# Two token mixers and a mixture of experts on one core: the gated layer with v ahead of u, and 40 unread products in three waits of the routing

## The reference, cut to what matters

```python
# h: (256, 1024)
z = gelu(rms_norm(h, ln_mix) @ c_w_in)              # 1024 x 2048, exact gelu
u, v = split(z, 2)                                  # 1024 columns each
v = layer_norm(v, c_ln_g, c_ln_b)                   # over the 1024 columns of a row
# in chunks of 128 positions, 8 groups of 128 columns; w_s lower-triangular
vs = einsum('gts,bnsgc->bntgc', w_s * tril, v) + b_s
h = h + (u * vs) @ c_w_out                          # 1024 x 1024
xt = rms_norm(h, ln_ffn)
logits = xt @ router_w                              # 1024 x 8
gates = softmax(top_2(logits))                      # two of eight experts for a token
h = h + moe(xt, gates)                              # rows sorted by expert
```

## Time and profile before

| | us |
|---|---|
| median of 3 runs | 2088.61 |
| lowest and highest run | 2087.92, 2090.22 |
| the profiled execution | 2090.02 |
| its span | 2088.3 |
| TensorE busy in the span | 1965.2 (94%) |
| VectorE busy | 1592.8 (76%) |
| ScalarE busy | 1194.4 (57%) |
| GpSimd busy | 28.1 (1%) |

### The profile page before, as it was taken

The page is one execution under the profiler, slowest core; times in us unless marked ns, Lnnn a source line. Parts: engine busy times, 40 slices in busy tenths (PEclk is TensorE's granted clock), DMA queues, the critical chain, the costliest instruction groups (busy, mean ns, idle before and its releaser), DMA issues.

```text
span 2088.3 us, 27813 instructions
## 1 busy us (share of the span) xinstructions
PE 1965.2 (94%) x11046; PEld 1693.1 (81%) x11046; DVE 1592.8 (76%) x1997; ACT 1194.4 (57%) x1638; POOL 28.1 (1%) x32
## 2 busy tenths in 40 slices
PE   8999999978999999999999999798999999989998
PEld 7889997767878787878787877687789988868997
DVE  5868886557898989898989898667479984856655
ACT  4543445425777777777777776556344444644443
POOL 0000000000000000000000000000000000000000
PEclk9999999988999999999999999899899999999999
DMA  7348884525898889898989998243158973214551
GB/s 301 133 156 349 336 332 158 207 75 218 336 350 334 340 345 341 340 343 338 342 341 342 340 343 332 102 142 122 41 195 334 359 280 123 104 44 164 183 184 59
DMA packets 71405, 512.02 MB, mean 245 GB/s; under 512 B 8162, under 2 KB 8546, under 8 KB 9826
## 3 DMA queue, kind: packets, MB, share of 16 engines
q1 hardware_dynamic: 69536, 504.40, 64.2%
q10 hardware_dynamic: 1732, 5.77, 0.8%
HBM read 509.08 MB, written 1.05 MB: 244 GB/s over the span
## 4 chain that ended last, share of the span: by engine, by line
PE 81%; DVE 12%; ACT 4%; issue 2%; POOL 1%; DMA 0%; POOLq 0%; ACTq 0%; DVEq 0%
PE ps L517 24%; PE ps L519 23%; PE ps L518 23%; DVE w_lo L1268 6%; ACT w_hi L2084 2%; PE ps L901 1%; PE ps L730 1%; PE ps L682 1%; PE ps L526 1%; PE ps L696 1%; PE ps L788 1%; PE ps L919 1%; POOL stat L2507 1%; PE ps L534 1%; ACT score L2192 1%
## 5 line engine op out<-in xcount | busy, mean ns | idle before, releaser
L1268 DVE TENSOR_TENSOR w_lo<-ring,w_hi 128x1024 fp32r<-128x1024 f32 x862 | 1046.1, 1225 | 344.7 <-ACT w_hi L2084 317.7
L2084 ACT ACTIVATE w_hi<-ring 128x1024 fp32r<-128x1024 f32 x862 | 913.0, 1062 | 667.8 <-PE ps L519 660.8
L517 PE MATMUL ps<-w_hi,x_hi 128*128 128x512 f32 (+1 forms) x1056 | 407.9, 389 | 6.6 <-DVE x_lo L1548 4.7
L519 PE MATMUL ps<-w_hi,x_lo 128*128 128x512 f32 (+1 forms) x1056 | 400.5, 382 | 0.0
L518 PE MATMUL ps<-w_lo,x_hi 128*128 128x512 f32 (+1 forms) x1056 | 399.7, 381 | 0.0
L517 PE MATMUL ps<-x_hi,w_hi 128*128 128x256 f32 x1248 | 360.4, 289 | 4.4 <-DVE x_lo L1382 3.9
L518 PE MATMUL ps<-x_lo,w_hi 128*128 128x256 f32 x1248 | 356.1, 285 | 0.0
L519 PE MATMUL ps<-x_hi,w_lo 128*128 128x256 f32 x1248 | 355.8, 285 | 0.0
L517 PE MATMUL ps<-w_hi,h_hi 128*128 128x512 f32 x732 | 292.0, 399 | 18.7 <-DVE h_lo L1837 15.7
L518 PE MATMUL ps<-w_lo,h_hi 128*128 128x512 f32 x732 | 285.7, 390 | 0.0
L519 PE MATMUL ps<-w_hi,h_lo 128*128 128x512 f32 x732 | 285.1, 389 | 0.0
(11 more groups left out here) (265 smaller groups left out, 1444.9 us busy)
## 6 DMA issues: line engine op xcount, KB each, us to landing
ring<-in_stream SPq DMA_DIRECT2D x479, 1024.0 KB, 4.9
con<-in_consts ACTq DMA_DIRECT2D x1, 2048.0 KB, 23.2
arena<-in_ln_rows ACTq DMA_DIRECT2D x3, 512.0 KB, 3.9
resid<-in_x SPq DMA_DIRECT2D x1, 1024.0 KB, 6.3
arena<-in_fin_row ACTq DMA_DIRECT2D x2, 512.0 KB, 3.5
out<-rows SPq DMA_DIRECT2D x2, 512.0 KB, 2.6
arena<-in_w_s ACTq DMA_DIRECT2D x1, 512.0 KB, 5.7
con<-in_consts ACTq DMA_DIRECT2D x1, 237.0 KB, 4.1
```

The costliest lines, as they stand in the source:

```text
L517: pe.matmul(out_, lhs[0], rhs[0], start=start, stop=False)
L519: return pe.matmul(out_, lhs[1], rhs[0], start=False, stop=stop)
L1268: dve.tensor_tensor(lo, ring[:, q % RING, a:a + HALF], hi.bitcast(F32), ALU.subtract)\
L2084: act.activation(half_buffer(m)[0], ring[:, q % RING, a:a + HALF], ACT.Copy).then_inc(hi_ready, 1)
```

## The change

- The stream and the kernel take the columns of v first (banks 0 to 3), then those of u (banks 4 to 7).
- TensorE takes the spatial product of rows 0 to 127 after five of u's eight halves, and that of rows 128 to 255 after the last three halves of u for t = 0; the last three halves of u go by rows: t = 0 for all three, then t = 1. The gated rows are transposed by t (`gated_transposes`): those of t = 0 before the last half of u for t = 1, those of t = 1 ahead of the third half of w_out for t = 0. The first three halves of w_out go by rows too, t = 0 behind the wait for `catT_kept` 4, t = 1 behind 6; then two whole halves, then `last_rows`.
- VectorE puts its splits of u's halves between the steps of the layer norm and the gating, ScalarE between the pieces of gelu. Gelu, x_hi, x_lo and gating go by t. New semaphores are `u_first` (u complete for t = 0) and `gated` (rows gated, one for each t, in place of `heads_ready`).
- `keep_warm` is called in three more waits: 18 products before the transposes of norm 4, 4 between these and the router, 18 between the router and the ranks. Bank 2 takes them; nobody reads them.

```diff
--- before.py
+++ after.py
@@ -390,6 +390,8 @@
         ple_gated = sem("ple_gated")
         gelu_done = sem("gelu_done")
         vn_ready = sem("vn_ready")
+        u_first = sem("u_first")
+        gated = sem("gated")
         ws_masked = sem("ws_masked")
         spatial_ready = sem("spatial_ready")
         logits_ready = sem("logits_ready")
@@ -536,7 +538,7 @@
                 def scaled(n):
                     pe.wait_ge(rows_scaled, 3 * k + n)
 
-                if k in (1, 6, 7, 9):
+                if k in (1, 4, 6, 7, 9):
                     keep_warm(18, 2)
                 scaled(1)
                 for f in range(4):
@@ -860,9 +862,10 @@
             rowsT(3)
             pe.wait_ge(ada_taken, 2)
             row_product(W_CIN, 0)
-            row_product(W_CIN + 4, 4)
-            pe.wait_ge(ws_masked, 1)
-            for t in range(QB):
+
+            def spatial(t):
+
+                pe.wait_ge(ws_masked, 1)
                 pe.wait_ge(vn_ready, t + 1)
                 for half in range(2):
                     for i in range(4):
@@ -870,12 +873,52 @@
                         last = pe.matmul(ps[:, 2 * t + half, i * P:(i + 1) * P], ws[:, g, :],
                                          v_rows[:, t, g * P:(g + 1) * P], start=True, stop=True)
                     last.then_inc(spatial_ready, 1)
-            pe.wait_ge(heads_ready, 2)
-            cat_transpose(8)
-            pe.wait_ge(catT_kept, 6)
-            row_product(W_COUT, 4, branch=True)
+
+            def gated_transposes(t):
+
+                pe.wait_ge(gated, t + 1)
+                for half in range(2):
+                    for i in range(4):
+                        f = 4 * half + i
+                        last = pe.transpose(ps[:, 2 * t + half, i * P:(i + 1) * P], rows[:, t, f * P:(f + 1) * P], ident)
+                    last.then_inc(catT_ready, 1)
+
+            u0, c0 = 2 * (W_CIN + 4), 2 * W_COUT
+            for k in range(5):
+                row_tile(u0 + k, (x_hi[:, k, :], x_lo[:, k, :]), 4, k == 0, False)
+            spatial(0)
+            w = []
+            for t in range(QB):
+                for k in range(5, KT):
+                    if t == 0:
+                        w.append(half_slot(u0 + k, 1))
+                    if (t, k) == (1, KT - 1):
+                        gated_transposes(0)
+                    row_part(w[k - 5], t, (x_hi[:, k, :], x_lo[:, k, :]), 4, False, k == KT - 1)
+                    if t == 1:
+                        row_end[0].then_inc(half_done, 1)
+                if t == 0:
+                    row_end[0].then_inc(u_first, 1)
+                    spatial(1)
+            pe.wait_ge(catT_kept, 4)
+            w = []
+            for t in range(QB):
+                if t == 1:
+                    pe.wait_ge(catT_kept, 6)
+                for k in range(3):
+                    if t == 0:
+                        w.append(half_slot(c0 + k, 1))
+                    if (t, k) == (0, 2):
+                        gated_transposes(1)
+                    row_part(w[k], t, (x_hi[:, k, :], x_lo[:, k, :]), 4, k == 0, False)
+                    if t == 1:
+                        row_end[0].then_inc(half_done, 1)
+            for k in (3, 4):
+                row_tile(c0 + k, (x_hi[:, k, :], x_lo[:, k, :]), 4, False, False)
+            last_rows(c0 + 5, [(x_hi[:, k, :], x_lo[:, k, :]) for k in range(5, KT)], 4, False)
 
             rowsT(4)
+            keep_warm(4, 2)
             pe.wait_ge(gained, GAINED_AT[4] + 4)
             for t in range(QB):
                 for k in range(KT):
@@ -883,6 +926,7 @@
                                      col("router", k * 8, 8), start=k == 0, stop=k == KT - 1)
             last.then_inc(logits_ready, 1)
 
+            keep_warm(18, 2)
             pe.wait_ge(member_ready, 1)
             pe.matmul(ps[:, 1, 0:8], col("before"), member[:, 0, :], start=True, stop=True)
             pe.matmul(ps[:, 1, 8:16], col("before"), member[:, 1, :], start=True, stop=False)
@@ -1203,7 +1247,7 @@
                 pe.wait_ge(cmp_kept, l + 1)
                 attention_rest(parts, TAIL, 12, 5)
                 pe.wait_ge(mixed_kept, GROUP_BASE[1 + l] + 12)
-                pe.wait_ge(heads_ready, 3 + l)
+                pe.wait_ge(heads_ready, 2 + l)
                 cat_transpose(8)
                 pe.wait_ge(catT_kept, 10 + 4 * l)
                 row_product(n0 + B_OUT, 4, branch=True)
@@ -1536,6 +1580,14 @@
                                              scalar=gain, in1=hi.bitcast(F32), op0=ALU.mult, op1=ALU.subtract)\
                         .then_inc(catT_kept, 1)
 
+            def keep_gated(t):
+
+                for half in range(2):
+                    dve.wait_ge(catT_hi, 2 + 2 * t + half + 1)
+                    at = slice(None), slice(4 * half, 4 * half + 4), slice(t * P, (t + 1) * P)
+                    dve.tensor_tensor(x_lo[at], ps[:, 2 * t + half, :].rearrange("p (f s) -> p f s", f=4),
+                                      x_hi[at].bitcast(F32), ALU.subtract).then_inc(catT_kept, 1)
+
             def keep_cat(count, before, gain=None):
 
                 for n in range(count):
@@ -1743,23 +1795,31 @@
             norm(3, gain(3), next_half=2 * W_CIN + 1, between=both_columns)
             for i in range(2):
                 scale_columns(0, i)
-            slots_done(W_COUT)
+            u0 = 2 * (W_CIN + 4)
+            split_to(reach(u0))
             for t in range(QB):
-                dve.wait_ge(gelu_done, 4 + 2 * t + 2)
+                dve.wait_ge(gelu_done, 2 * t + 2)
                 for half in range(2):
                     ins = dve.bn_stats(bn[:, t, half, :], v_rows[:, t, half * BANK:(half + 1) * BANK])
                 link(ins)
                 link(dve.bn_aggr(mv[:, t, :], bn[:, t].rearrange("p a b -> p (a b)")))
                 link(dve.tensor_copy(stat[:, 8 + t:9 + t], mv[:, t, 1:2]))
-            root(stat[:, 8:10], 2, 1.0, LN_EPS)
+            dve.tensor_scalar(stat[:, 0:2], stat[:, 8:10], 1.0, LN_EPS, ALU.mult, ALU.add).then_inc(root_asked, 1)
+            roots[0] += 1
+            split_to(reach(u0 + 1))
+            dve.wait_ge(root_ready, roots[0])
             dve.wait_ge(ln_in, 16 * 3)
             for t in range(QB):
+                split_to(reach(u0 + 2 * t + 1))
                 link(dve.tensor_scalar(v_rows[:, t, :], v_rows[:, t, :], mv[:, t, 0:1], stat[:, t:t + 1],
                                        ALU.subtract, ALU.mult))
                 link(dve.tensor_tensor(v_rows[:, t, :], v_rows[:, t, :], ln_g, ALU.mult))
+                split_to(reach(u0 + 2 * t + 2))
                 dve.tensor_tensor(v_rows[:, t, :], v_rows[:, t, :], ln_b, ALU.add).then_inc(vn_ready, 1)
+            split_to(reach(u0 + 5))
             for t in range(QB):
                 for half in range(2):
+                    dve.wait_ge(gelu_done, 4 + 2 * t + half + 1)
                     dve.wait_ge(spatial_ready, 2 * t + half + 1)
                     for i in range(4):
                         g = 4 * half + i
@@ -1767,8 +1827,11 @@
                                                        in0=ps[:, 2 * t + half, i * P:(i + 1) * P],
                                                        scalar=col("bs", g, 1), in1=u_rows[:, t, g * P:(g + 1) * P],
                                                        op0=ALU.add, op1=ALU.mult)
-            ins.then_inc(heads_ready, 1)
-            keep_cat(4, 2)
+                ins.then_inc(gated, 1)
+                split_to(reach(u0 + 6 + 2 * t))
+                keep_gated(t)
+                if t == 0:
+                    split_to(reach(u0 + 7))
             add_branch(4, W_COUT + 4, first_half=1)
             norm(4, gain(4))
             dve.wait_ge(logits_ready, 1)
@@ -2297,14 +2360,36 @@
             act.dma_start(ln_g, ln_rows[0].partition_broadcast(P)).then_inc(ln_in, 16)
             act.dma_start(ln_b, ln_rows[1].partition_broadcast(P)).then_inc(ln_in, 16)
             act.dma_start(ws, w_s).then_inc(ln_in, 16)
-            for part, dst in enumerate((u_rows, v_rows)):
-                slots_done(W_CIN + 4 * part + 4)
-                for b in range(4):
-                    act.activation(dst[:, b // 2, (b % 2) * BANK:(b % 2 + 1) * BANK], ps[:, 4 * part + b, :], ACT.Gelu)\
+            def gelu(dst, b0, t):
+
+                for half in range(2):
+                    act.activation(dst[:, t, half * BANK:(half + 1) * BANK], ps[:, b0 + 2 * t + half, :], ACT.Gelu)\
                         .then_inc(gelu_done, 1)
+
+            def keep_gated(t):
+
+                for half in range(2):
+                    act.wait_ge(catT_ready, 2 + 2 * t + half + 1)
+                    act.activation(x_hi[:, 4 * half:4 * half + 4, t * P:(t + 1) * P],
+                                   ps[:, 2 * t + half, :].rearrange("p (f s) -> p f s", f=4), ACT.Copy).then_inc(catT_hi, 1)
+
+            u0 = 2 * (W_CIN + 4)
+            split_to(reach(u0 - 1))
+            act.wait_ge(half_done, u0)
+            gelu(v_rows, 0, 0)
```

(14 more changed lines are left out.)

## The result

The changed kernel takes 0.9934 of the time before (95% interval 0.9917 to 0.9951), which is 13.8 us less (10.2 to 17.3). Its runs were 2071.02, 2075.77 and 2076.95 us; a fourth, of 4637.05 us, was disturbed and the comparison leaves it out. The forecast was 2072.3 us for the median, which is 2075.77 us, and 2073.7 us for a profiled execution, whose time was 2076.95 us with a span of 2074.8 us.

The account below looks back on a forecast made before the run. TensorE bounds nearly throughout, so only its standstills or low clock (1.2 instead of 2.4 GHz) can give time. Gated layer 10.8 plus routing 5.5 is 16.3 us, from 2088.6 to a median of 2072.3 us; range 2066.5 to 2080.0.

Parts of the forecast that it names:

- Both stretches: Gated layer (21.6 us, last w_in half to first w_out product) and routing (31.4 us): the only ones that could give time.
- Gated layer: v ahead of u, halves by rows: upper bound 16.1 us less 5.3 us of new waits, a gain of 10.8 us.
- TensorE's own work: Gated layer: spatial products 3.5 us at full clock and transposes 2.0 us, together 5.5 us.
- The table load: Ahead of the first gelu, ScalarE: 1.28 us, hidden before 392.74; if it came after the wait, gain 9.5 us.
- the signs that the forecast named: If right: first w_out product near 422, last over near 447, experts' first near 473, router passes 0.11 us apart.
- Routing: 40 unread products in three waits keep the clock up: gain 5.5 us, bounds 1 and 7.5.
- Router: Routing, 32 passes of 8 columns: 3.5 instead of 7.0 us, the last pass or two perhaps slow; gain 3.2 us.
- three falls: Earlier clock falls came 3.1, 3.8 and 4.7 us after TensorE's last wide product; the router would end 4.2 us after.
- Last 18 ahead of the ranks: Unread products between router and ranks, partly at half rate: ranks 1.2 to 1.7 us late, taken as -0.9 us.
- Gather: End of routing: 6.02 us become 3.74 if the clock holds, 5.4 if it drops at the start; gain 1.7 us.
- the clock is not kept in the routing: Rival, routing: narrow work doesn't hold the clock, routing gains only 2.1 us, total 2075.7 us; chance 0.15.
- The rival in which splits become the bound: u and w_out halves: each waits for its whole split, 36.8 us, total 2103.8 us; decides from 1.35 us per half; chance 0.02.

Follow-up runs that it names:

- e1: The changed kernel without its 40 unread products (new gated layer, routing of before): ratio 0.9946, gated layer 75.75 us, routing 32.23 us.
- e2: The kernel before with only the 40 unread products in three waits of the routing: ratio 0.9968, routing 25.31 us.
- e4: The changed kernel with u in whole halves, spatial products and both sets of transposes behind all of u: ratio 0.9948, gated layer 82.94 us.
- e7: The changed kernel with the last 18 unread products replaced by ten fp32 products of 8 columns (20 passes): ratio 0.9946, routing 29.42 us.
- e3: The changed kernel without the last 18 unread products, between router and ranks: ratio 0.9927, routing 29.42 us.
- e6: The changed kernel with two more unread products between the router's two blocks of rows: ratio 0.9942, routing 27.44 us.

## Why the prediction was right, and where its terms were off

**The reading of the bound held.** Both stretches named as the only ones with anything to give gave 11.20 and 4.66 us, and `e1` and `e2` show that the two gains stand apart: the gated layer takes 75.75 us with and without the unread products, and these shorten the routing with the old layer too.

**Gated layer, 10.8 forecast, 11.2 measured.** TensorE's own work between the whole halves was 5.5 us in the forecast. Measured: the spatial products put 2 x 1.70 us on the path (409.34 to 411.04 and 415.74 to 417.44), the transposes 0.79 and 0.85, 5.0 us together. The waits, as the distance between product starts less a slot of 0.227 us (for 427.79, the same up to the transposes' start):

| ahead of | forecast | measured |
|---|---|---|
| u's fourth half (402.51) | 0.4 | 0.09 |
| fifth half (406.44) | 0.9 | 1.07 |
| eighth half (414.23) | 1.1 | 0.37 |
| w_out, first rows' x_lo (423.45) | 0.8 | 0.91 |
| second transposes (427.79) | 1.9 | 1.46 |
| w_out, second rows' x_lo (430.45) | 0.2 | 0.34 |
| sum | 5.3 | 4.2 |

Each stands where it was laid and each was ended by the step named. On top comes what I had left out: the second product after every restart came 0.31 to 0.35 us behind the first instead of 0.227 (406.44 and 406.79, for one), ten restarts from v's first product on, some 1.0 us, of which the two of before have 0.2. With the other 0.8 the stops cost 5.0 us, next to the 5.3 forecast, so the sum is better than its terms, and that is luck: the waits came 1.1 us under the forecast, TensorE's own work 0.5 us under it, and the restarts were not in it. The table load did hide: it ran ahead of the wait for v.

```profile
392.88 1.28 ACT L2366 ACT_TABLE_LOAD   x1
394.46 1.09 ACT L2366 ACTIVATE arena<-ps 128x512 f32<-128x512 f32 x2 [0.30 <-PE ps L521]
```

By the 2.66 us that the Trainium skill (ScalarE: Activation LUTs, What ACT_TABLE_LOAD costs) gives for load and drain, the fourth half would have been later by about 1 us, as an estimate; the row shows the gelu 1.58 us behind the load's start, of which the last 0.30 is a wait for TensorE, and the fourth half 0.09 us late. The root on GpSimd beside a split took 1.60 us (401.42), as the 1.47 of the earlier trace rows had it.

Of the signs that the forecast named, the first w_out product is at 423.45 and the last at 448.14; less the 1.77 us by which this execution was late before the gated layer, that is 421.7 and 446.4, where 422 and 447 stood. The experts' first product is at 475.08, so 473.3 where 473 stood. The router's passes are not 0.11 us apart throughout, and one of the signs of being wrong is there in part: the last 18 unread products ran 0.43 us apart until the clock was back at 464.5.

**Routing, 5.5 forecast, 4.66 measured, 6.3 in `e2` and `e4`.** Term by term:

- Router's start: 0.66 us earlier, forecast 0.4.
- Router: 6.99 to 5.47, so 1.5 us where 3.2 stood. This is the term that was mis-sized. The step that had it wrong was that the clock outlasts the last wide product by 3.1 to 4.7 us. In the change it fell 2.5 us after the last unread product's end (455.2 to 457.7), sooner than in any of the three falls that the forecast went by, and sixteen passes ran at full rate instead of thirty. In the eleven traces with the first two groups the fall came 2.3 (`e7`) to 4.8 us (`e2`) after them. In the ten traces with the first two groups of unread products and nothing between the router's blocks, the router took 3.74 us (twice), 3.86, 4.28, 4.52, 4.70 and four times 5.46 to 5.63. So this term has no one size: it changes from one execution to the next, 4.70 and 5.47 in two of the same code. That the routing's sum came out within 0.9 us is luck in part: the gather and the router's earlier start gave 0.7 us more than forecast and made up for some of the 1.7 us that the router gave less.
- Last 18 ahead of the ranks: forecast -0.9. The first rank product started 0.89 us after `most` was written (466.97 against 466.02 + 0.06), and the 18 took 5.84 us.
- Ranks and selection, up to the gather: 3.99 to 2.86, 1.1 us, as forecast.
- Gather: 6.02 to 3.84, 2.2 us, forecast 1.7; the clock held to its end.

The three falls were also not alike. The forecast says that the fall at 462.5 came with transposes running, and takes it for a sign that narrow work doesn't hold the clock. In the trace of before TensorE had stood still for most of that time: 2.71 us ahead of four transposes, then 1.02 us ahead of the others, which began 0.1 us before the fall (462.34 in the earlier trace rows).

```profile
460.67 0.66 PE L534 MATMUL ps<-con,rows 128*128 128x128 f32 x4 [2.71 <-DVE rows L1337]
```

The fall at 418.1 came in the 10.3 us wait, so only the one at 360.05 had narrow work ahead of it throughout. What the forecast inferred from the wrong row is shown by the runs: with passes of 8 columns alone the clock fell in `e3` and `e7`, and in `e7` it did not come back while they ran.

**The rival "the clock is not kept in the routing"** (2.1 us there) was half right. The clock fell, with the engine busy on narrow passes, but the gather was at full rate all the same: behind the last 18 the clock was back, and in `e3` and `e7`, without them, it was not. The Trainium skill (TensorE: Matmul & The Clock Gate, Part 4: PE-mode transpose) says that transposes don't count as a busy engine for the clock; `e7` shows the like for ordinary products with 8 columns, 20 passes in 4.42 us with the clock at 0.50 before, in and behind them. For transposes by themselves no run here tests it, the fall at 462.5 included. The rival in which splits become the bound would have shown over 1.35 us of wait for each half; the largest was 1.46 and the mean over sixteen 0.26.

**The 2.4 us that went elsewhere.** The +1.77 us ahead of v's first product began in the first attention block, whose code is the same. Windows of before, then of after:

```profile
102.00:103.00 1.00, 0.62 (x6) 0.62 (x7) 1.00 (x2) 0.00 (x0) 0.63 (x1) 1.00 1.01 426
103.00:104.00 1.00, 1.00 (x11) 1.00 (x10) 0.67 (x2) 0.93 (x2) 0.00 (x0) 1.00 0.51 213
...
102.00:103.00 1.00, 0.36 (x2) 0.36 (x3) 1.00 (x2) 0.00 (x0) 0.89 (x1) 0.84 0.98 418
103.00:104.00 1.00, 1.00 (x7) 1.00 (x6) 0.72 (x1) 0.21 (x1) 0.00 (x0) 0.50 0.74 311
```

In the execution of after the clock was at 0.50 while those transposes ran. Such falls come and go in unchanged code: the stretch behind the routing lay between 1591.8 and 1604.1 us over the fourteen traces. Runs of one kernel differ along with them. Of `e2`'s twelve runs, the four with a mean clock of 0.978 took 2075.3 to 2076.8 us, six with 0.972 to 0.976 took 2079.6 to 2085.9, and two with 0.971 took 2090.3 and 2090.8. A mean lower by 0.007 is some 29 us more at the lower level (0.014 of 2080 us), which can cost up to 15 us, as much as these groups lie apart. What draws one outcome or the other, in the router and elsewhere, no run here settles.

## What to carry to other kernels

When a chain of VectorE (statistics, root, norm, gate) follows a product and another independent product of the same layer is still to come, take the one that feeds the chain first, and sweep the second by blocks of rows, so that each block's chain runs beside products of the other; a wait that this removes may be worth more than its length where the clock falls in it (in `e4` the waits were 3.5 us longer and the layer some 6 us, with the start's 1.1 us taken off). In TensorE's queue put work whose inputs are ready ahead of a wait for something later: one such turn gave 1.06 us in the trace. Unread wide products paid here directly ahead of narrow work, in waits about as long as they are (6.3 us of the routing in `e2`, 2.5 us for the last 18 in the traces, not shown in the median). Where the clock may have fallen before them, price them at half rate: the last 18 took 5.8 to 7.0 us here, against 4.25 at full clock. Don't count on a few of them among narrow passes to keep the clock.

## What the runs showed of the hardware that I had not expected

- The clock fell 2.5 us after the last wide product (455.2 to 457.7), though TensorE had been idle for only 0.59 us of them, and in the same router in `e2` and `e4` not before its last pass (32 passes in 3.74 us).
- Ordinary fp32 products with 8 columns, 4.42 us of them back to back, left the granted clock at 0.50, while the clock came back 3.2 us into 18 products with 512 columns (461.29 to 464.5).
- Two wide products at full clock between narrow ones did not keep it (3.15 us for the next 16 passes, 1.95 for those before; `e6`).
- After a stop of TensorE the second 512-column product comes 0.31 to 0.35 us behind the first instead of 0.227, also where the stop was a change to narrow passes and back.
